# One-hot weights that stand still in the gather of a mixture of experts, and a third early place for its weights

## The chip, the cores and the metric

The kernel runs on one core of a Trainium2 chip. The metric is device time in microseconds (us). A measurement of this kernel is a few executions of the program, and the median is given.

## What is computed

One encoder layer over 256 tokens of width 1024: a projection, a group of gated linear attention heads beside a group of softmax attention heads, an output projection, and then a mixture of experts with 32 experts of which each token takes 4. The part that matters here is the mixture:

```python
h = h + moe_ffn(rms_norm(h, ffn_norm_g), w_router, b_router, w1, b1, w2, b2)
# moe_ffn: top-4 of 32 experts for each token, and for the tokens of expert e
h = xb @ w1[e] + b1[e]                       # xb: gathered tokens; 1024 x 2048 weights
h_glu = minimum(h[:, :1024], 7.0); h_lin = clip(h[:, 1024:], -7.0, 7.0)
act = h_glu * sigmoid(1.702 * h_glu) * (h_lin + 1.0)
y = act @ w2[e] + b2[e]                      # 1024 x 1024 weights, added back with the token's gate
```

All weights are float32. An expert has 12 MB of them, and 32 experts have 403 MB, which is nearly all that the kernel reads.

## The kernel before

It is written by hand, engine by engine, with semaphores. Each engine's program is in the order in which the code emits it.

**The stages.** The front (projection, both attentions, output projection, router) takes about 140 us. Then the 32 experts run one after the other, each for up to 64 tokens (`CAP`). At the end the sum is normalised and stored.

**Weights.** The weights of an expert come in six chunks of 2 MB (128 partitions x 4096 floats, `SLOT`): chunks 0 to 3 are `w1`, chunks 4 and 5 `w2`. Chunks are numbered through, so chunk 6e is the first one of expert e. The tile `ring` has eight slots (`SLOTS`). SyncE (SP) issues all transfers in the order of the chunks. TensorE (PE) counts `chunk_used` up when it has multiplied with a chunk, and SP waits for that count before it loads over a slot. During the front most of the ring holds other things, and SP waits for semaphores of the front before it loads each of the first eight slots (`first_ring`). `EARLY` is the number of chunks that go to a place outside the ring, in the tile `work`, while the front still runs: these are chunks 19 and 20 (`EARLY_AT` is 19). The number of used chunks that SP waits for before it loads chunk c over a slot is c-7 up to chunk 18, c-9 for the chunks 21 to 28 (`SLOTS + EARLY` behind), and c-7 again from chunk 29 on, since the early places are used once (`refill_first`, `PEELED`). From expert 8 on SP loads pairs of chunks (4 MB at a time, L399), each when both chunks before it in its two slots have been used.

**One expert on PE.** `start_hidden` adds the bias. L1642 multiplies the gathered tokens `xg` with four chunks of `w1`: 32 matmuls with 64 columns of stationary operand and 512 columns moving, two matmul instructions for each float32 matmul. Then `gather(n + 1)` fetches the tokens of the next expert (L1544), `combine` adds the result of the expert before (L1556), four transposes turn the hidden values (L1668, they wait for VectorE's `hid_ready`), two turn the gates (L1677), and L1686 multiplies with the two chunks of `w2`, after ScalarE has copied the turned hidden values (`hidT_sb`, L624).

**The gather.** Token rows are split into three bf16 parts (`parts`, `PARTS` is 3) whose sum is the normalised float32 value. For each of 8 blocks of features, 3 parts and 2 tiles of tokens, the part is the stationary operand (128 x 128) and the one-hot matrix of the expert (64 columns) moves: 48 matmuls in bf16. The result stands in bank 6 already turned, with features on the partitions, and VectorE writes it to `xg` with the gain (L1066). The parts are made on ScalarE, VectorE and GpSimd between the router and the first expert (L596, L606, L611, L994, L1006, L1012, L454, L456). `xg` needs features in the order `(m r)` with r running over 4 rows of the weights in one partition (`W1_RUN`), so every use of token rows steps over 4 elements.

**The first gather** is done in two halves (`first_gather`, L1530, and `half_out`, L1074), since the first chunk needs only half of `xg`. It stands ahead of the first L1642 but for its last quarter, which stands behind chunk 0.

## Time and profile before

| | |
|---|---|
| median of 3 runs | 1055.63 us (1055.35 to 1057.44) |
| the profiled execution | 1055.04 us, of which the span of the profile is 1053.3 us |
| PE busy | 985.9 us (94%) |
| VectorE (DVE) busy, ScalarE (ACT) busy | 223.6 us (21%), 119.1 us (11%) |
| read from HBM | 419.95 MB, 400 GB/s over the span |
| granted clock of PE | 0.986 of full speed on average |

Instructions have the line of the program that emits them. Times in views are in us from the start of the span. A view by windows gives the busy time of PE, of PE's weight loads (PEld), DVE, ACT and GpSimd (POOL), the granted clock of PE as a share of full speed, the mean busy share of the 16 DMA engines and what they moved. The chain of work that ended last is followed back from the end of the program; a piece of it is what the piece after it had to wait for.

### The profile page before, as it was taken

The page shows a single profiled execution, that of the slowest core. Times are in us where ns is not written, and L with a number is a line of the kernel's source. Part 1 is how long each engine was busy: PE and PEld are TensorE (multiplying, and loading weights), DVE is VectorE, ACT ScalarE, POOL GpSimd, SP SyncE. Part 2 cuts the span into 40 slices and gives each one's busy share as a digit, 9 for nine tenths or more (in the row PEclk, how much of TensorE's full clock was granted, in tenths as well). Part 3 has the DMA queues.
Part 4 walks back from the last instruction along what each step waited for, and adds up shares of the span by engine and source line. Part 5 has one row for each costly group of instructions (what it writes and reads, how often), then busy time and mean ns, then how long its engine had stood idle before and what let it go on. Part 6 is the DMA issues. An engine that isn't in the chain of part 4 may idle for free.

```text
span 1053.3 us, 13569 instructions
## 1 busy us (share of the span) xinstructions
PE 985.9 (94%) x5863; PEld 438.2 (42%) x5863; DVE 223.6 (21%) x525; ACT 119.1 (11%) x235; POOL 17.3 (2%) x19
## 2 busy tenths in 40 slices
PE   7999999999999999999989899989999889999896
PEld 6646444444343444444333343333343334343332
DVE  1786351111011111111111110111111111010112
ACT  1054130000000000000000000000000000000002
POOL 0010110000000000000000000000000000000000
PEclk9999999999999999999999999999999999999998
DMA  9927769999999999999999999999999999999995
GB/s 356 265 77 320 340 262 430 426 427 423 429 425 433 424 431 428 432 435 424 436 436 424 434 436 426 434 434 429 431 434 433 427 436 434 423 427 427 427 425 205
DMA packets 25233, 421.50 MB, mean 400 GB/s; under 512 B 4176, under 2 KB 4688, under 8 KB 6800
## 3 DMA queue, kind: packets, MB, share of 16 engines
q1 hardware_dynamic: 25200, 421.01, 94.9%
q8 instruction: 26, 0.43, 0.2%
q14 instruction: 7, 0.06, 0.0%
HBM read 419.95 MB, written 1.05 MB: 400 GB/s over the span
## 4 chain that ended last, share of the span: by engine, by line
PE 65%; DMA 30%; ACT 2%; DVE 2%; issue 1%; POOL 1%; SPq 0%; POOLq 0%; DVEq 0%
DMA ring<-in_w_dram 30%; PE bank L1642 29%; PE bank L1686 14%; PE bank L1556 4%; PE bank L1544 3%; PE bank L1206 3%; PE bank L1668 1%; PE bank L1447 1%; PE bank L1278 1%; ACT work L624 1%; PE bank L1375 1%; PE bank L1472 1%; PE bank L1602 1%; PE bank L1247 1%; POOL stat L428 1%
## 5 line engine op out<-in xcount | busy, mean ns | idle before, releaser
L1642 PE MATMUL bank<-ring,work 128*64 128x512 f32 x2016 | 459.7, 608 | 33.1 <-DMA ring<-in_w_dram 33.0
L1642 PEld LDWEIGHTS bank<-ring,work 128*64 128x64 f32 x2016 | 175.8, 139 | 297.0 <-issue 238.1
L1686 PE MATMUL bank<-ring,work 128*64 128x512 f32 x992 | 219.7, 595 | 14.9 <-ACT work L624 14.9
L1090 DVE TENSOR_SCALAR work<-bank 128x512 f32<-128x512 f32 x31 | 21.4, 691 | 685.0 <-PE bank L1642 685.0
L1686 PEld LDWEIGHTS bank<-ring,work 128*64 128x64 f32 x992 | 68.9, 137 | 145.8 <-issue 127.5
L621 ACT ACTIVATE work<-work 128x512 f32<-128x512 f32 x31 | 19.7, 634 | 499.1 <-DVE work L1090 499.1
L1556 PE MATMUL bank<-work 64*128 64x512 f32 x256 | 63.6, 615 | 0.7 <-ACT work L656 0.7
L1544 PE MATMUL bank<-work,tok 128*128 128x64 bf16 x992 | 51.2, 197 | 0.0
L1544 PE MATMUL bank<-work 128*128 128x64 bf16 x496 | 50.0, 197 | 0.0
L1544 PEld LDWEIGHTS bank<-work,tok 128*128 128x128 bf16 x992 | 48.8, 116 | 0.0
L1544 PEld LDWEIGHTS bank<-work 128*128 128x128 bf16 x496 | 36.5, 115 | 24.8 <-issue 24.8
L632 ACT ACTIVATE work<-bank 128x512 f32<-128x512 f32 x31 | 18.5, 597 | 214.7 <-PE bank L1686 214.7
L1556 PEld LDWEIGHTS bank<-work 64*128 64x128 f32 x256 | 22.0, 186 | 18.7 <-issue 15.9
L624 ACT ACTIVATE work<-bank 128x512 f32<-128x512 f32 x31 | 18.5, 597 | 91.6 <-PE bank L1668 91.6
L1668 PEld LDWEIGHTS bank<-ckeep,work 128*128 128x128 f32 x124 | 17.3, 210 | 24.0 <-DVE work L1096 22.5
L1083 DVE TENSOR_SCALAR work<-ckeep,work 128x128 f32<-128x128 f32 x62 | 18.7, 344 | 34.8 <-PE bank L1677 34.8
L428 POOL TENSOR_TENSOR stat<-stat 128x1 f32<-128x1 f32 (+2 forms) x8 | 9.7, 1212 | 955.7 <-DVE stat L683 939.3
L1668 PE MATMUL bank<-ckeep,work 128*128 128x128 f32 x124 | 23.2, 310 | 1.2 <-DVE work L1096 1.2
L1093 DVE SCALAR_TENSOR_TENSOR work<-work 128x512 f32<-128x512 f32 x31 | 21.5, 692 | 1.1
L1096 DVE TENSOR_TENSOR work<-work 128x512 f32<-128x512 f32 x31 | 21.5, 692 | 1.1
L1066 DVE TENSOR_TENSOR work<-bank,ffn_pairs 128x512 f32<-128x512 f32 x31 | 21.2, 683 | 0.0
L1091 DVE TENSOR_SCALAR work<-bank 128x512 f32<-128x512 f32 x31 | 21.1, 680 | 0.0
(221 smaller groups left out, 503.5 us busy)
## 6 DMA issues: line engine op xcount, KB each, us to landing
ring<-in_w_dram SPq DMA_DIRECT2D x60, 4096.0 KB, 29.1
ring<-in_w_dram SPq DMA_DIRECT2D x67, 2048.0 KB, 15.1
ring<-in_w_in_dram SPq DMA_DIRECT2D x8, 1168.0 KB, 15.2
ring<-in_w_dram SPq DMA_DIRECT2D x6, 1024.0 KB, 34.1
work<-in_w_dram SPq DMA_DIRECT2D x2, 2048.0 KB, 14.7
ring<-in_w_out_dram SPq DMA_DIRECT2D x2, 1024.0 KB, 10.5
ring<-in_w_out_dram SPq DMA_DIRECT2D x1, 2048.0 KB, 16.7
h<-in_x_dram SPq DMA_DIRECT2D x2, 512.0 KB, 4.2
```

The lines of the kernel that those rows point to most:

```text
L624: nc.scalar.activation(hidT, bank[5][:, :].rearrange("p (s q) -> p s q", q=P), ACT.Copy)\
L1066: nc.vector.tensor_tensor(xg.rearrange("p (k c) -> p k c", c=CAP), bank[6][:, :].rearrange("p (k c) -> p k c", c=CAP), ffn_pairs.rearrange ...
L1090: nc.vector.tensor_scalar(glu, bank[2][:, :], LIMIT, None, ALU.min).then_inc(S.glu_ready, 1)
L1091: nc.vector.tensor_scalar(lin, bank[5][:, :], LIMIT, -LIMIT, ALU.min, ALU.max).then_inc(S.dve_step, 1)
L1093: nc.vector.scalar_tensor_tensor(lin, lin, 1.0, glu, ALU.add, ALU.mult).then_inc(S.dve_step, 1)
L1096: nc.vector.tensor_tensor(lin, lin, sig, ALU.mult).then_inc(S.hid_ready, 1)
L1206: return mm(o, l, r, start=a and first, stop=z, skip_group_check=True)
L1544: last = mm(bank[6][:, k * CAP:(k + 1) * CAP], rows_of(t, i, k), onehot[:, t, :], start=i == 0 and t == 0, stop=i == PARTS - 1 and t == TI ...
L1556: last = mm(bank[Y[i]][:, :], gatedT[j * CAP:(j + 1) * CAP, t, :], res[j * CAP:(j + 1) * CAP, :], start=start, stop=stop, skip_group_check ...
L1642: last = mm(bank[(2, 5)[g]][j * CAP:(j + 1) * CAP, :], xg[:, k * CAP:(k + 1) * CAP], of_group(chunk[:, r, :], g, j), start=False, stop=k = ...
L1668: last = nc.tensor.transpose(bank[5][:, r * P:(r + 1) * P], apart[:, :, r], ident)
L1686: last = mm(bank[6][j * CAP:(j + 1) * CAP, :], hidT[:, r, s * CAP:(s + 1) * CAP], chunk[:, r, j * 512:(j + 1) * 512], start=s == 0 and r == 0,
```

## The change

The one-hot matrix becomes float32, has the factor 1/rms of each token in its columns, and is now the stationary operand. The float32 token rows `h` move past it, 512 columns at a time: 2 tiles of tokens by 2 halves of the features are 4 float32 matmuls, with tokens of the expert on the partitions of bank 6. ScalarE copies bank 6 to `rows_sb` (the same place as `glu`, so it waits for `hid_ready` too), PE turns it in 4 transposes into bank 2 (`turn_rows`, behind L1677), and VectorE writes `xg` from there. The sigmoid is written to bank 2, and no longer to `sig`. The bf16 parts, and what makes them, are gone.

The place that this frees holds a third early chunk, chunk 21 (`EARLY` is 3), in two halves of 1 MB: one in `tok`, one in `work`. SP loads it behind `first_ring(6)`, after the attention output has been turned (`glaT_ps`). SP now waits for c-10 used chunks before chunk c for the chunks 22 to 29, and for c-7 from chunk 30 on. `TURN` moves the numbering of the slots by one, so that the ring is in step with the pairs. `res`, `gated` and the second half of `hT` move to other places.

```diff
-EARLY = 2
+EARLY = 3
+TURN = 1
+        early_rows = [tok.rearrange("p t d -> p (t d)"), work[:, at_split:at_split + SLOT // W1_ROWS]]
...
         def slot_of(c):
-            return (c - EARLY) % SLOTS
+            return (c - EARLY + TURN) % SLOTS
...
+            def load_split(i):
+                e, r = divmod(EARLY_AT + i, PER_EXPERT)
+                n = SLOT // W1_ROWS
+                for j in range(W1_ROWS):
+                    at = r % PAIR * SLOT + j * n
+                    sp.dma_start(early_rows[j], rows_of(e, r)[:, at:at + n]).then_inc(early_in[i], 16)
...
-            for i in range(EARLY):
+            for i in range(EARLY - 1):
                 load_early(i)
             sp.wait_ge(S.att_used, 1)
             first_ring(6)
+            sp.wait_ge(S.glaT_ps, TILES)
+            load_split(EARLY - 1)
             sp.wait_ge(S.h_ps, 2 * TILES)
             first_ring(7)
...
+            def rows_out(n):
+                act.wait_ge(S.gathered, n + 1)
+                act.wait_ge(S.hid_ready, n)
+                nc.scalar.activation(rows_sb, bank[6][:, :], ACT.Copy).then_inc(S.rows_done, 1)
...
-                nc.scalar.activation(sig, glu, ACT.Sigmoid, scale=ALPHA).then_inc(S.sig_ready, 1)
+                nc.scalar.activation(bank[2][:, :], glu, ACT.Sigmoid, scale=ALPHA).then_inc(S.sig_ready, 1)
+                rows_out(n + 1)
...
             def gathered_out(n):
-                dve.wait_ge(S.gathered, n + 1)
+                dve.wait_ge(S.turned_ps, n + 1)
...
-            left_over(0)
             first_mask(0)
             first_mask(1)
-            last_part(0)
+            half_rows_out()
             half_out(0, 3)
-            left_over(1)
-            last_part(1)
             tables()
...
+            def interleaved(t, nb, r0, n):
+                return h[:, t, nb * 512:(nb + 1) * 512].rearrange("p (m r) -> p r m", r=W1_RUN)[:, r0:r0 + n, :]
...
             def gather(n):
-                for k in range(KD):
-                    for i in range(PARTS):
-                        for t in range(TILES):
-                            last = mm(bank[6][:, k * CAP:(k + 1) * CAP], rows_of(t, i, k), onehot[:, t, :],
-                                      start=i == 0 and t == 0, stop=i == PARTS - 1 and t == TILES - 1)
+                for t in range(TILES):
+                    for j in range(GROUPS):
+                        last = mm(bank[6][j * CAP:(j + 1) * CAP, :], onehot[:, t, :], interleaved(t, j, 0, W1_RUN),
+                                  start=t == 0, stop=t == TILES - 1, skip_group_check=True)
+            def turn_rows(n):
+                pe.wait_ge(S.rows_done, n + 1)
+                for r in range(W1_RUN):
+                    last = nc.tensor.transpose(bank[2][:, r * P:(r + 1) * P], rows_sb[:, r * P:(r + 1) * P], ident)
+                last.then_inc(S.turned_ps, 1)
...
                 last.then_inc(S.gatedT_ps, 1)
+                turn_rows(n + 1)
                 pe.wait_ge(S.hidT_sb, n + 1)
-                pe.wait_ge(S.xg_ready, n + 2)
...
             first_gather(0, 0)
             first_gather(0, 1)
             first_gather(1, 0)
+            turn_first(0)
+            first_gather(1, 1)
```

**PE behind the first layer of expert 1.** Before, from `gather(2)` (L1544, 48 matmuls; of its rows, which repeat in this pattern, the first and the last ones stand here) to the first chunk of `w2`:

```order
L1544 MATMUL bank<-work 128x64 [waits res_ready,xg_ready,onehot_ready]
L1544 MATMUL bank<-work 128x64
L1544 MATMUL bank<-work,tok 128x64 x4
...
L1556 MATMUL bank<-work 128x512 [waits extra_done,res_ready]
L1556 MATMUL bank<-work 128x512 x3
L1668 MATMUL bank<-ckeep,work 128x128 [waits hid_ready]
L1668 MATMUL bank<-ckeep,work 128x128 x3
L1677 MATMUL bank<-ckeep,work 128x128 [waits gatedT_sb,gated_ready]
L1677 MATMUL bank<-ckeep,work 128x128
L1686 MATMUL bank<-ring,work 64x512 [waits slot_in2,xg_ready,hidT_sb]
```

The same stretch of the change, where L1537 is the gather, L1555 `combine` and L1544 the new `turn_rows`:

```order
L1537 MATMUL bank<-h,work 64x512 [waits res_ready,xg_ready,onehot_ready]
L1537 MATMUL bank<-h,work 64x512 x3
L1555 MATMUL bank<-work 128x512 [waits extra_done,res_ready]
L1555 MATMUL bank<-work 128x512 x3
L1668 MATMUL bank<-ckeep,work 128x128 [waits hid_ready]
L1668 MATMUL bank<-ckeep,work 128x128 x3
L1677 MATMUL bank<-ckeep,wr_sb 128x128 [waits gatedT_sb,gated_ready]
L1677 MATMUL bank<-ckeep,wr_sb 128x128
L1544 MATMUL bank<-ckeep,work 128x128 [waits rows_done]
L1544 MATMUL bank<-ckeep,work 128x128 x3
L1686 MATMUL bank<-ring,work 64x512 [waits slot_in3,hidT_sb]
```

48 small matmuls have become 4 large ones, and 4 transposes stand between L1677 and L1686.

**SP at the end of the front.** Before, from the two early chunks to the first refills that wait for `chunk_used`:

```order
L347 DMA work<-in_w_dram 128x4096 [waits ogla_ps]
L347 DMA work<-in_w_dram 128x4096
L347 DMA ring<-in_w_dram 128x4096 [waits att_used]
L347 DMA ring<-in_w_dram 128x4096 [waits h_ps]
L347 DMA ring<-in_w_dram 128x4096 [waits chunk_used] x38
```

The change:

```order
L345 DMA work<-in_w_dram 128x4096 [waits ogla_ps]
L345 DMA work<-in_w_dram 128x4096
L345 DMA ring<-in_w_dram 128x4096 [waits att_used]
L367 DMA tok<-in_w_dram 128x2048 [waits glaT_ps]
L367 DMA work<-in_w_dram 128x2048
L345 DMA ring<-in_w_dram 128x4096 [waits h_ps]
L345 DMA ring<-in_w_dram 128x4096 [waits chunk_used] x37
```

Two transfers of half a chunk come ahead of the last slot of the ring, and one refill fewer waits for `chunk_used`.

**PE at the first gather.** The change, from the filler matmuls (L1470) to the first chunk (L1642); L1518 is `first_gather` and L1527 `turn_first`:

```order
L1470 MATMUL bank<-h,ckeep 128x128 x4
L1518 MATMUL bank<-h,work 64x256 [waits onehot_first]
L1518 MATMUL bank<-h,work 64x256
L1518 MATMUL bank<-h,work 64x256 [waits onehot_ready]
L1518 MATMUL bank<-h,work 64x256
L1518 MATMUL bank<-h,work 64x256 [waits onehot_first]
L1518 MATMUL bank<-h,work 64x256
L1527 MATMUL bank<-ckeep,work 128x128 [waits half_rows]
L1527 MATMUL bank<-ckeep,work 128x128
L1518 MATMUL bank<-h,work 64x256 [waits onehot_ready]
L1518 MATMUL bank<-h,work 64x256
L1642 MATMUL bank<-ring,work 64x512 [waits slot_in1,half_xg]
```

Before, 36 matmuls in bf16 (L1530) stood ahead of the first L1642 and 12 behind chunk 0, and no transposes. Now the second half's two transposes stand behind chunk 0.

## Rows read from the trace of the kernel before

**Rows 1.** The page: busy time by engine, and the chain by engine.

```profile
PE 985.9 (94%) x5863; PEld 438.2 (42%) x5863; DVE 223.6 (21%) x525; ACT 119.1 (11%) x235; POOL 17.3 (2%) x19
...
PE 65%; DMA 30%; ACT 2%; DVE 2%; issue 1%; POOL 1%; SPq 0%; POOLq 0%; DVEq 0%
```

**Rows 2.** Windows: PE, PEld, DVE, ACT, POOL, then PEclk, DMA share, GB/s.

```profile
126.00:134.00 8.00, 8.00 (x43) 4.12 (x45) 3.39 (x7) 3.56 (x7) 1.66 (x3) 1.00 0.03 10
...
140.00:145.00 5.00, 4.67 (x42) 2.04 (x39) 2.67 (x7) 3.13 (x5) 0.00 (x0) 1.00 0.03 11
...
150.00:240.00 90.00, 86.97 (x572) 38.58 (x570) 18.00 (x43) 7.81 (x15) 0.00 (x0) 1.00 1.01 426
```

**Rows 3.** The chain in expert 1: start, us, what.

```profile
168.28 13.79 PE bank L1642 x64
182.07 1.67 PE bank L1544 x48
183.74 1.92 PE bank L1556 x8
185.66 0.69 PE bank L1668 x4
186.38 0.61 ACT work L624
...
187.03 7.09 PE bank L1686 x32
194.11 0.46 PE bank L1472 x4
```

**Rows 4.** The chain where PE waits for weights: two experts apart.

```profile
560.64 7.14 PE bank L1642 x32
...
618.93 7.14 PE bank L1642 x32
```

**Rows 5.** SP's timeline: issues at three places, start and us.

```profile
234.67 0.33 SPq L347 DMA_DIRECT2D ring<-in_w_dram  x1
...
243.30 0.33 SPq L347 DMA_DIRECT2D ring<-in_w_dram  x1
...
361.57 0.33 SPq L399 DMA_DIRECT2D ring<-in_w_dram  x1
```

**Rows 6.** DMA issues: KB, us to landing; windows at 144.5, 234, 243, 361.

```profile
ring<-in_w_dram SPq DMA_DIRECT2D x1, 2048.0 KB, 7.4
...
ring<-in_w_dram SPq DMA_DIRECT2D x1, 2048.0 KB, 12.9
...
ring<-in_w_dram SPq DMA_DIRECT2D x1, 2048.0 KB, 9.1
...
ring<-in_w_dram SPq DMA_DIRECT2D x1, 4096.0 KB, 14.3
```

**Rows 7.** Timeline of expert 1 between its two layers.

```profile
184.15 0.69 DVE L1096 TENSOR_TENSOR work<-work 128x512 f32<-128x512 f32 x1
...
186.18 0.38 PE L1677 MATMUL bank<-ckeep,work 128*128 128x128 f32 x2
...
187.03 1.51 PE L1686 MATMUL bank<-ring,work 128*64 128x512 f32 x6 [0.47 <-ACT work L624]
```

**Rows 8.** Weight loads of L1668 and L1677: ns min/median/max.

```profile
L1668 PEld LDWEIGHTS bank<-ckeep,work x124: 195/209/223, 159.3 to 1007.4; 128*128 128x128 f32 x124
...
L1677 PEld LDWEIGHTS bank<-ckeep,work x62: 141/146/153, 159.8 to 1007.6; 128*128 128x128 f32 x62
```

**Rows 9.** Timeline of the first gather.

```profile
138.31 1.14 PE L1478 MATMUL bank<-h,ckeep 128*128 128x128 f32 x8
...
140.71 0.42 DVE L1074 TENSOR_TENSOR work<-bank,ffn_pairs 128x256 f32<-128x256 f32 x1 [0.42 <-PE bank L1530]
...
141.19 3.71 PE L1642 MATMUL bank<-ring,work 128*64 128x512 f32 x16
```

**Rows 10.** PE's timeline in the last expert.

```profile
1024.29 7.14 PE L1642 MATMUL bank<-ring,work 128*64 128x512 f32 x32 [1.19 <-DMA ring<-in_w_dram]
```

More of the change, by code:

```diff
@@ L219, in encoder_layer @@
         w_out_gla = ring[:, 7 * SLOT:8 * SLOT].rearrange("p (k n) -> p k n", n=D)
-        early = [work[:, KD * SEQ + i * SLOT:KD * SEQ + (i + 1) * SLOT] for i in range(EARLY)]
+        early = [work[:, KD * SEQ + i * SLOT:KD * SEQ + (i + 1) * SLOT] for i in range(EARLY - 1)]
+        at_split = KD * SEQ + (EARLY - 1) * SLOT
+        early_rows = [tok.rearrange("p t d -> p (t d)"), work[:, at_split:at_split + SLOT // W1_ROWS]]
         back = Carve(work)
@@ L240, in encoder_layer @@
         lin = back(FG)
-        sig = back(FG)
-        hidT = back(SUB, P)
-        part0 = back(TILES * D // 2).bitcast(BF16).rearrange("p (t d) -> p t d", d=D)
+        rows_sb = glu
         part_sb = back(TILES, P)
         gateT = part_sb.rearrange("p t c -> p (t c)")
-        res = back(D // GROUPS)
-        reuse = Carve(work, at_glu)
-        left = reuse(TILES, D)
+        hidT = back(SUB, P)
+        left = Carve(work, at_split)(TILES, D)
         assert back.at <= WORK
         b1_wide = tok.rearrange("p t d -> p (t d)")
-        parts12 = tok.bitcast(BF16).rearrange("p t (i d) -> p t i d", i=PARTS - 1)
-        parts = [[part0[:, t, :]] + [parts12[:, t, i, :] for i in range(PARTS - 1)] for t in range(TILES)]
-        hT = [turned[:, :, 0:P], tok[:, 1, :].rearrange("p (k t) -> p k t", t=P)]
+        hT = [turned[:, :, 0:P], Carve(work, at_glu)(KD, P)]
         ffn_pairs = sb("ffn_pairs", [P, KD])
@@ L992, in _ @@
             turned_out(0, 0, 0)
-            dve.wait_ge(S.part0_t0, 1)
-            nc.vector.scalar_tensor_tensor(left[:, 0, :], h[:, 0, :], stat[:, 4:5], parts[0][0], ALU.mult, ALU.subtract)\
-                .then_inc(S.left_t0, 1)
             add_h(1, 1)
@@ L1634, in expert @@
                     fine = final and c in FINE
-                    chunk = by_row(slot_for(q, c) if fine else loaded(q, c, it, final_body), 2 * FF)
+                    chunk = slot_for(q, c) if fine else loaded(q, c, it, final_body)
                     for r in range(W1_ROWS):
@@ L1642, in expert @@
                                 last = mm(bank[(2, 5)[g]][j * CAP:(j + 1) * CAP, :], xg[:, k * CAP:(k + 1) * CAP],
-                                          of_group(chunk[:, r, :], g, j), start=False, stop=k == KD - 1,
+                                          of_group(row_of(chunk, r, 2 * FF), g, j), start=False, stop=k == KD - 1,
                                           skip_group_check=True)
@@ L1686, in expert @@
                             last = mm(bank[6][j * CAP:(j + 1) * CAP, :], hidT[:, r, s * CAP:(s + 1) * CAP],
-                                      chunk[:, r, j * 512:(j + 1) * 512], start=s == 0 and r == 0,
+                                      row_of(chunk, r, D)[:, j * 512:(j + 1) * 512], start=s == 0 and r == 0,
                                       stop=s == W2_CHUNKS - 1 and r == W2_ROWS - 1, skip_group_check=True)
```

127 lines of the change are left out of this document (56 added, 71 removed).

## The prediction

> **What bounds the kernel now.** I read the page first. PE is busy for 94% of the span, and 65% of the chain that ended last is PE and 30% DMA [rows 1]. So neither is the bound alone, and I ask where each is. The windows answer. The DMA engines stand still from 126 to 134 us (share 0.03) and from 140 to 145 us (0.03), and from 150 us on they never do (1.01, 426 GB/s) [rows 2]. Two experts of PE in the second half of the kernel are 618.93 - 560.64 = 58.3 us apart, 29.15 us each or 4.86 us for a chunk of 2 MB [rows 4]. That is the pace of the DMA. PE's own pace is that of expert 1, where it waits for no weights: 13.79 + 1.67 + 1.92 + 0.69 + 0.61 + 0.04 + 7.09 + 0.46 = 26.3 us [rows 3], where 0.04 is the hand-over from ScalarE. So PE is 2.9 us an expert faster than the DMA, lives on what was loaded ahead as long as that lasts, and then waits for weights. The end comes from the DMA: in the last expert PE waited 1.19 us for a chunk, and nothing behind that waits for weights again [rows 10].
>
> From this alone the answer would be simple: every microsecond in which the DMA stands still before 145 us is lost, and the third early place fills 4.86 of them. But a place helps only as long as the DMA always has somewhere to put the next chunk. So I read SP's issues against their landings. The first refill, issued at 144.9 us when the queue is empty [rows 2], lands after 7.4 us [rows 6]; that is 4.86 us of data and 2.5 us around them. The load issued at 234.67 us (chunk 29) lands 12.9 us later, at 247.6, and the one issued at 243.30 (chunk 30) lands 9.1 us later, at 252.4 [rows 5, 6]. The second was issued only 4.3 us before the first had landed. It would have landed as early if issued 9.1 - 7.4 = 1.7 us later, and not more. The ring is nearly full there: SP waited for PE to finish chunk 22. The next narrow place is the pair issued at 361.57 us, which lands after 14.3 us [rows 5, 6]. A pair on an empty queue would take 7.4 + 4.86 = 12.3, so the slack there is 2.0 us. I read all other issues from 170 to 470 us the same way, and all have more. Those of the first expert, before 170 us, have little too, but there the loads themselves will start later (below).
>
> **The change part by part.** *The third place.* It is issued behind the last slot but one and has landed before the last slot is issued: the queue is empty for 8 us from 126 on [rows 2], and 2 MB are 4.86 us. So chunk 21 costs nothing and one refill fewer is left: -4.86 us on the side of the DMA.
>
> *Where that gain meets the ring.* Chunks 22 to 29 now go out at the counts of 21 to 28 before. So chunk 29 lands where chunk 28 did, about 242.7. Chunk 30 still waits for chunk 22 to be used: its count is c-7 before and after. It is issued at 243.30 plus whatever PE has lost by then, and lands 7.4 us later, at 250.7 plus that loss, instead of at 252.4. **So of 4.86 us only 1.7 minus PE's loss remain**, and the DMA stands still for 3 us that it did not before. At 361.57 the same holds with 2.0. What counts is therefore what PE loses in its first four and first eight experts.
>
> *PE's loss in each expert.* The gather: 48 matmuls cost 1.67 us now [rows 3]. It becomes 4 float32 matmuls with 64 stationary columns and 512 moving, the form of L1642 and L1686, 8 instructions. L1642 needs 13.79 / 64 = 0.215 us for each of its instructions, so 8 cost 1.72 us: +0.05. What no row shows is such a matmul whose moving operand steps over 4 floats (16 bytes). The nearest row is L1668, which loads a 128 x 128 operand with this step as weights: 209 ns for one against 146 ns for L1677 without it [rows 8]. But the loads overlap. In pace the step costs little: L1668 begins at 185.66 and L1677 at 186.18 [rows 3, 7], 0.13 us for each of four, or 1.02 ns a column. In L1642 two streams run side by side, so each has 0.43 us for 512 columns, 0.84 ns. At 1.02 the gather costs 4 x 0.52 = 2.09 us: +0.42. I take +0.1, nearer to L1642, since that row is the same form but for the step, and since L1668's pace has the moving of 128 more columns in it.
>
> *The four transposes* stand between L1677 and L1686. By L1668's pace four cost 4 x 0.13 = 0.52 us. PE idles 0.47 us there anyway, waiting for ScalarE's copy L624 [rows 7]. They nearly fit. Their own wait (`rows_done`) is over by then: VectorE's L1096 ends at 184.84 [rows 7], ScalarE's new copy of 0.61 us (the size of L624) ends at 185.5, and the next thing on ScalarE, L624, is due at 186.38 [rows 3]. If the cover went, they would cost 0.52 us. Behind the transposes VectorE has all of L1686 (7.09 us) to write `xg`. I take 0.05 for this, so 0.15 us an expert in all (0.05 to 0.47 by the bounds).
>
> *The first gather.* Removed are the splits into parts, which lie beside PE but for the last one. New are, in line: a copy of 256 columns, two transposes and their hand-overs. L1642's 16 instructions take 3.71 us [rows 9], 0.27 more than 16 x 0.215, which is the drain of the last. So the filler matmuls end their issue at 138.31 + 1.14 - 0.27 = 139.2 [rows 9]. Eight instructions of 256 columns at 0.11 and the drain end at 140.4. The copy (0.42, as L1074), two transposes (0.38, as L1677) and L1074 itself (0.42) with four hand-overs of 0.04 end at 141.8. L1642 began at 141.19 [rows 9], so chunk 0 begins 0.6 us later. Behind it two transposes stand where 12 matmuls did, and a quarter of the gather has moved under L1074: about 0.4 us comes back. 0.2 us is left for the rest.
>
> *Sum.* At the first narrow place PE is 0.2 + 4 x 0.15 = 0.8 us late, so 1.7 - 0.8 = 0.9 us of gain. At the second it is 0.2 + 8 x 0.15 = 1.4 late, so 2.0 - 1.4 = 0.6 us. The smaller one decides: -0.6 us. Later the slack grows by 2.9 us an expert and the loss by 0.15. PE still needs only 26.5 us for an expert, less than the 29.15 of the DMA, and in the last expert the 1.19 us of waiting cover 0.15 [rows 10]. So the profiled execution would go from 1055.04 (span 1053.3 and 1.7 around it) to 1054.4, and the median, 0.6 above the profiled one, from 1055.63 to about 1055.0. 0.2% of this kernel is 2.1 us, about what a measurement can tell from no change.
>
> **The rivals.** *The whole chunk is gained* (chance 0.10). For it: the DMA share is 1.01 all along and the engines stand still at the front [rows 2]. Then the time falls by 4.86 less the 0.6 us by which the first refill is later: 4.3, to 1051.3. Against it stands the pair of issue and landing at 243.30. It needs PE to reach chunk 22 at least 2.6 us earlier than now, and nothing in the change is shorter on PE.
>
> *The stepping operand is slow* (0.18, slower than before). Two streams read the same partitions side by side, each element from another place. If each column pays the 63 ns / 128 = 0.49 ns by which the stepping load is longer [rows 8], one instruction takes 0.43 + 0.25 = 0.68 us and the gather 4 x 0.68 = 2.72 us: +1.05 an expert and +0.3 in the first gather. Then the second narrow place costs 0.5 + 8 x 1.05 - 2.0 = +6.9 us: 1062.5. It decides from 0.23 us an expert on, where 0.2 + 8 x 0.23 = 2.0, and can be measured from 0.5 on. At twice the time for each column it is +1.76 an expert and 12.6 us: 1068. Against it: 48 matmuls of L1544, each with a load of 128 stepping bf16 columns, follow each other at 1.67 / 48 = 0.035 us [rows 3], so PE can read stepping data fast. The Trainium skill has a rule for this, in Advanced Engine Details and Errata, section SBUF Cachelines: accesses that hit the same 16-byte line run at full speed, at least two hits on a line are needed, and another line for each access has a penalty. It gives no size. By that rule the new operand, with one float in each line, would be slow; the longer load in L1668 agrees, its pace hardly.
>
> *The turn is not hidden* (0.10). The transposes come late because ScalarE's copy pushes L624 back, or the hand-overs do not overlap: 0.52 + 0.1 us an expert. 0.2 + 8 x 0.62 - 2.0 = +3.2: 1058.8. Against it: between the end of the copy and L624 there are 0.9 us, by the times above.
>
> **How the numbers follow.** The forecast (the ring is full at chunk 30, PE loses 0.05 to 0.47 an expert) has 0.62, and its own range is 1054.3 to 1057.6: at 0.05 an expert the first place leaves 1.7 - 0.4 = 1.3 of gain and the second 1.4; at 0.47 the second costs 0.2 + 3.8 - 2.0 = 2.0. The range of 8 in 10 is 1053.5 to 1062.5: it leaves out most of the full gain below and the slower half of the stepping operand above. Faster by over 0.2%: 0.10 and 0.02 of the forecast, 0.12. Slower: 0.18 and 0.10 and a little of the forecast, 0.30. Within: 0.58.
>
> **What would show it.** In the profile of the changed kernel the refill on SP near 244 us should be issued to an empty queue (7.4 us to landing), with DMA share near 0.6 for some 4 us there, and full otherwise. The gather should be 8 instructions in 1.7 to 1.9 us, and 2.7 or more if the rival holds. The wait of L1686 for ScalarE should be near 0. PE should begin to wait for weights about one expert later. The prediction is wrong if the DMA never stands still behind 150 us (then the whole chunk is gained), or if one expert of PE takes more than 26.6 us.

## The result, and the profile after

The changed kernel takes 1070.87 us (median of 4 runs, 1070.42 to 1072.33). The kernel before took 1056.24 beside it, so the ratio is 1.0142, with a 95% interval of 1.0130 to 1.0154. I had forecast 1055.0 and a range up to 1062.5. The profiled execution took 1070.75, with a span of 1068.6.

The page of the changed kernel, busy time and the chain by engine:

```profile
PE 1046.7 (98%) x4719; PEld 427.3 (40%) x4719; DVE 224.2 (21%) x521; ACT 133.3 (12%) x262; POOL 13.8 (1%) x17
...
PE 82%; DMA 13%; DVE 2%; SPq 1%; issue 1%; ACT 1%; POOL 0%; POOLq 0%; DVEq 0%
```

PE is busy 61 us longer with 1144 instructions fewer (31 gathers at 1.97 us more, as shown below, make 61), and the chain has moved from the DMA to PE [rows 1]. The chain of one expert says where, in the columns of [rows 3]. L1537 is the gather, L1555 the combine, L1544 the four new transposes, L1464 the next bias rows:

```profile
185.41 3.64 PE bank L1537 x8
189.05 1.92 PE bank L1555 x8
190.97 0.68 PE bank L1668 x4
191.65 0.22 PE bank L1677 x2
191.87 0.44 PE bank L1544 x4
192.30 0.03 issue
192.33 7.09 PE bank L1686 x32
199.42 0.45 PE bank L1464 x4
199.87 13.79 PE bank L1642 x64
```

Line by line against [rows 3]: the gather takes 3.64 us instead of 1.67. L1677 and the new transposes (0.22 + 0.44 + 0.03) stand where the chain went through ScalarE's copy L624 (0.02 + 0.61 + 0.04). All else is as before. One gather begins 28.25 us behind the other (185.41, 213.66), where an expert took 26.3. One row of the view of L1537 (ns min, median, max) shows the size for each instruction; L1642 and L1686, of the same form without the step, have 592:

```profile
L1537 PE MATMUL bank<-h,work x248: 1059/1079/1117, 158.9 to 1022.1; 128*64 128x512 f32 x124
```

The front, that is the chain up to the first expert (L1470 is the filler matmuls, whose result nobody uses, L1518 the first gather, L1527 its transposes):

```profile
138.09 1.76 PE bank L1470 x8
139.86 2.89 PE bank L1518 x12
142.74 0.37 PE bank L1527 x2
143.11 1.03 PE bank L1518 x4
144.15 3.49 PE bank L1642 x16
```

The first matmul of the first expert is at 143.96 (its first records stand under the gather's drain), 2.8 us behind [rows 9].

Now the ring. SP's issues of chunk 30 and of the pair that went out at 361.57 before, then the DMA's view of the two (KB, us to landing), then windows in the columns of [rows 2]:

```profile
252.50 3.76 SPq L345 DMA_DIRECT2D ring<-in_w_dram  x2
...
378.93 0.33 SPq L408 DMA_DIRECT2D ring<-in_w_dram  x1
```

```profile
ring<-in_w_dram SPq DMA_DIRECT2D x1, 2048.0 KB, 7.3
...
ring<-in_w_dram SPq DMA_DIRECT2D x1, 4096.0 KB, 13.0
```

```profile
245.00:250.00 5.00, 4.97 (x26) 2.34 (x26) 0.85 (x2) 1.47 (x3) 0.00 (x0) 1.00 0.00 0
250.00:257.00 7.00, 7.00 (x36) 2.48 (x34) 1.05 (x4) 0.60 (x1) 0.00 (x0) 1.00 0.53 187
```

The DMA engines stand still for some 7 us before 252.5 (the load before landed at 245.7), since the ring is full and PE has not finished chunk 22. Then the load lands 7.3 us after its issue, as on an empty queue [rows 6]. The pair goes out 17.36 us later than in [rows 5] and lands 13.0 us later, at 391.9: 16.1 us behind the kernel before, where it landed at 375.9. In the last expert the same shift stands: the chunk that landed at 1024.2 lands at 1040.3. PE begins with it 16.4 us later than before, at 1040.71 against 1024.29 [rows 10], since PE itself is now 0.4 us behind that landing and no longer waits for it.

### The profile page after: what moved, and what is told of

Same layout as the page of the kernel before. It is cut to its first block, busy times and chain, and to the rows that moved or that the text cites. A ratio compares the mean times of both kernels' runs of the same rounds, so it can differ in the third digit from the quotient of the medians.

```text
span 1068.6 us, 11333 instructions
## 1 busy us (share of the span) xinstructions
PE 1046.7 (98%) x4719; PEld 427.3 (40%) x4719; DVE 224.2 (21%) x521; ACT 133.3 (12%) x262; POOL 13.8 (1%) x17
## 3 DMA queue, kind: packets, MB, share of 16 engines
HBM read 419.95 MB, written 1.05 MB: 394 GB/s over the span
## 4 chain that ended last, share of the span: by engine, by line
PE 82%; DMA 13%; DVE 2%; SPq 1%; issue 1%; ACT 1%; POOL 0%; POOLq 0%; DVEq 0%
PE bank L1642 36%; PE bank L1686 18%; DMA ring<-in_w_dram 11%; PE bank L1537 9%; PE bank L1555 5%; DMA tok<-in_b_dram 2%; PE bank L1668 2%; PE bank L1439 1%; PE bank L1270 1%; PE bank L1464 1%; PE bank L1367 1%; PE bank L1544 1%; PE bank L1602 1%; DVE tok L734 1%; PE bank L1239 1%
## 5 line engine op out<-in xcount | busy, mean ns | idle before, releaser
L1642 PE MATMUL bank<-ring,work 128*64 128x512 f32 x2000 | 440.0, 594 | 3.3 <-DMA ring<-in_w_dram 3.3
L1642 PEld LDWEIGHTS bank<-ring,work 128*64 128x64 f32 x2000 | 176.3, 136 | 247.8 <-issue 231.4
L1686 PE MATMUL bank<-ring,work 128*64 128x512 f32 x992 | 219.7, 595 | 1.4
L1686 PEld LDWEIGHTS bank<-ring,work 128*64 128x64 f32 x992 | 68.8, 137 | 132.2 <-issue 125.3
L1537 PE MATMUL bank<-h,work 128*64 128x512 f32 x248 | 119.2, 1082 | 0.0
L623 ACT ACTIVATE bank<-work 128x512 f32<-128x512 f32 x31 | 18.7, 602 | 457.2 <-DVE work L1084 457.2
L1555 PE MATMUL bank<-work 64*128 64x512 f32 x256 | 63.6, 615 | 0.7 <-ACT work L660 0.7
L1555 PEld LDWEIGHTS bank<-work 64*128 64x128 f32 x256 | 22.0, 186 | 70.1 <-issue 68.5
L1537 PEld LDWEIGHTS bank<-h,work 128*64 128x64 f32 x248 | 24.6, 146 | 58.8 <-issue 58.8
L636 ACT ACTIVATE work<-bank 128x512 f32<-128x512 f32 x31 | 18.5, 598 | 214.7 <-PE bank L1686 214.7
L618 ACT ACTIVATE work<-bank 128x512 f32<-128x512 f32 x31 | 18.5, 597 | 73.7 <-PE bank L1537 73.7
L1668 PEld LDWEIGHTS bank<-ckeep,work 128*128 128x128 f32 x124 | 17.3, 209 | 24.5 <-issue 22.7
L628 ACT ACTIVATE work<-bank 128x512 f32<-128x512 f32 x31 | 18.5, 597 | 60.0 <-PE bank L1668 59.9
L1668 PE MATMUL bank<-ckeep,work 128*128 128x128 f32 x124 | 23.2, 309 | 0.0
L1090 DVE TENSOR_TENSOR work<-work,bank 128x512 f32<-128x512 f32 x31 | 21.3, 687 | 1.1
L1464 PE MATMUL bank<-biases,sel 96*64 96x512 bf16 x128 | 20.0, 390 | 0.0
L1198 PE MATMUL bank<-ring,work 128*128 128x32 f32 (+2 forms) x80 | 19.3, 391 | 0.0
## 6 DMA issues: line engine op xcount, KB each, us to landing
ring<-in_w_in_dram SPq DMA_DIRECT2D x8, 1168.0 KB, 15.3
```

Source lines behind the costliest of these rows:

```text
L1090: nc.vector.tensor_tensor(lin, lin, bank[2][:, :], ALU.mult).then_inc(S.hid_ready, 1)
L1198: return mm(o, l, r, start=a and first, stop=z, skip_group_check=True)
L1464: mm(bank[(2, 5)[g]][j * CAP:(j + 1) * CAP, :], sel, of_group(b1_parts, g, j), start=True, stop=False, skip_group_check=True)
L1537: last = mm(bank[6][j * CAP:(j + 1) * CAP, :], onehot[:, t, :], interleaved(t, j, 0, W1_RUN), start=t == 0, stop=t == TILES - 1, skip_grou ...
L1555: last = mm(bank[Y[i]][:, :], gatedT[j * CAP:(j + 1) * CAP, t, :], res[j * CAP:(j + 1) * CAP, :], start=start, stop=stop, skip_group_check ...
L1642: last = mm(bank[(2, 5)[g]][j * CAP:(j + 1) * CAP, :], xg[:, k * CAP:(k + 1) * CAP], of_group(row_of(chunk, r, 2 * FF), g, j), start=False ...
```

## The experiments

Each run is the changed kernel with one more edit. Times are medians; all ran beside the kernel before, whose medians were 1055.92 to 1056.37 us. That kernel scatters from 1054 to 1061, so I lean on traces where less than 1 us is in question.

### What makes the gather slow

**m1_pace** puts ten groups of eight matmuls behind PE's last instruction. The profile shows an instruction as a record; each matmul gives two records in float32 and one in bf16. One group, shortened (`streams` is 1 or 2, and `moving` picks the columns):

```
for i in range(8):
    j, t = i % streams, i // streams % 2
    mm(bank[5][j * CAP:(j + 1) * CAP, 0:256], weights, moving(t), start=True, stop=True)
```

> The changed kernel with ten groups of eight matmuls behind TensorE's last instruction (their result is not used). Each matmul has 256 columns of moving operand; what varies is whether the columns stand side by side, every second, every fourth or every eighth one (f32 from h, bf16 from the biases), and whether all eight go to the same half of the output partitions (one stream) or alternate between the two halves (two streams). In the changed kernel's gather, f32 with every fourth column and two streams, an instruction of 512 columns takes 0.455 us of the chain, and side by side 0.2155 us: for 256 columns 0.228 and 0.108 us. Theory A, the step slows each stream by itself: f32 step four costs about twice the plain group both with one stream (0.43 to 0.46 us against 0.2155 us an instruction) and with two. Theory B, two streams share one reader that fetches a stepped column in about 0.9 ns: f32 step four costs 0.228 us an instruction with one stream as with two, and one stream loses nothing to plain. Theory C, the step is not the cause (it is reading h in f32, or the one-hot in f32): plain and stepped groups take the same. For the size of the step, A and B both leave open whether step two (8 bytes) lies halfway or with step four, and whether bf16 with step eight (16 bytes) behaves as f32 with step four.

The chain at its end (a count of 15 is a group of 16 records of which one stands in a neighbouring piece). Float32: L1717 and L1720 are side by side with one and two streams, L1723 step two with one stream, L1729 and L1732 step four with one and two. Bf16, one stream: L1735 side by side, L1738 step four, L1741 step eight.

```profile
1061.70 3.38 PE bank L1717 x15
...
1065.30 1.73 PE bank L1720 x15
1067.02 3.40 PE bank L1723 x15
...
1072.47 6.77 PE bank L1729 x15
...
1079.69 3.62 PE bank L1732 x15
1083.32 0.88 PE bank L1735 x8
1084.19 1.81 PE bank L1738 x8
1086.00 3.61 PE bank L1741 x8
```

Divide the second number by the count. Float32 side by side takes 0.225 us a record, step two 0.227, step four 0.451; with two streams 0.115 and 0.241. So theory A holds: the step slows each stream by itself, and two streams still run side by side. Bf16 takes 0.110, 0.226 and 0.451 for spans of 2, 8 and 16 bytes. In one stream that is 0.43, 0.88 and 1.76 ns a column. The granted clock was 1.00 in the stretches of all these groups but the last, where it was 0.94.

**m2_spans** asks how far this goes, with 128 columns and one stream.

> The changed kernel with eleven groups of eight matmuls behind TensorE's last instruction (their result is not used). The first eight groups move 128 columns in one stream: f32 side by side, pairs out of four, step four, eight, sixteen; bf16 step two, four, sixteen. In the earlier trial (256 columns, one stream) a record took 0.226 us for f32 side by side and step two, 0.451 for step four, 0.110 for bf16 side by side, 0.226 for step four, 0.451 for step eight. Theory (a column costs the bytes of row that it spans, about 9 bytes in a ns, and never less than its own pace): pairs of four as plain, 0.113 us; step four 0.225; step eight 0.45 and step sixteen 0.9 us if the span goes on counting; bf16 step two 0.055, step four 0.113, step sixteen 0.9. Rival (from 16 bytes on every column is a fetch of its own at 1.76 ns): step eight and sixteen 0.225 us as step four, bf16 step sixteen 0.225. The last three groups load 128 columns of h as stationary operand, side by side, step four and step eight, and move 64: whether a stepped load slows them as well; from the changed kernel's rows (a load of 209 ns stepped, 146 ns not, for transposes) 0.17 us against 0.11 us a record is expected at most.

L1716 moves pairs out of four, L1718 step four, L1720 step eight, L1722 step sixteen (float32); L1724 step two, L1728 step sixteen (bf16). L1730 and L1734 load h as weights, side by side and with step eight, and move 64 columns.

```profile
1063.38 1.81 PE bank L1716 x16
1065.19 3.63 PE bank L1718 x16
1068.82 3.72 PE bank L1720 x16
1072.53 3.48 PE bank L1722 x16
1076.01 0.46 PE bank L1724 x8
...
1077.40 1.86 PE bank L1728 x8
1079.26 3.40 PE bank L1730 x16
...
1086.38 3.84 PE bank L1734 x16
```

The rival holds: 0.227, 0.232 and 0.217 us for steps of 16, 32 and 64 bytes, so a column costs 1.7 to 1.8 ns in all three. Pairs out of four are as fast as plain (0.113), and so is bf16 with step two (0.058 us for 128 columns, half of 0.110 and a little).

The weights need more care. A stepped load of weights takes 0.24 us a record against 0.21, 13% more, but the granted clock was 1.00 up to 1079.2 us and 0.50, the lower level of 1.2 GHz, from 1080 us on:

```profile
1080.00:1090.00 10.00, 10.00 (x45) 10.00 (x44) 0.00 (x0) 0.00 (x0) 0.00 (x0) 0.50 0.00 0
```

So these groups don't tell what the step costs in the weights at full speed. The next run does: there one load takes 209 ns with the step and 140 without, and four transposes 0.48 us instead of 0.44, 9% more. The moving side pays 100%.

**e1_contiguous** moves the step from the gather to the transposes, in experts 1 to 31 (lines shortened).

```diff
-  mm(bank[6][j * CAP:(j + 1) * CAP, :], onehot[:, t, :], interleaved(t, j, 0, W1_RUN), ...)
+  mm(bank[6][j * CAP:(j + 1) * CAP, :], onehot[:, t, :], h[:, t, j * 512:(j + 1) * 512], ...)
-  nc.tensor.transpose(bank[2][:, r * P:(r + 1) * P], rows_sb[:, r * P:(r + 1) * P], ident)
+  nc.tensor.transpose(bank[2][:, r * P:(r + 1) * P], rows_sb.rearrange("p (m r) -> p r m", r=W1_RUN)[:, r, :], ident)
```

> The changed kernel, but the gather of experts 1 to 31 moves 512 columns of h that stand side by side, and the step of four is in the transposes behind it, which read the picked rows with a step as stationary operand. The first expert's gather still steps. Theory (the stepped moving operand costs the time): the eight gather instructions take 1.72 to 1.80 us of the chain where they took 3.64, the four transposes 0.6 to 0.7 where they took 0.44, an expert on TensorE 26.4 to 26.6 us where it took 28.26, and with 1.6 us lost at the first expert and 8 x 0.2 up to the gate at the pair issue, minus 2.0 of slack, the time is 1056 to 1058 us. Rival (the f32 one-hot or h itself makes the gather slow): the gather stays at 3.6 us and the time at 1070 to 1071.

1057.71 us, ratio 1.0005 (0.9993 to 1.0017). Its chain:

```profile
184.86 1.72 PE bank L1537 x8
...
189.39 0.48 PE bank L1544 x4
...
211.18 1.72 PE bank L1537 x8
```

The gather is back at 1.72, the transposes cost 0.04 more, and an expert takes 26.32 us. One address pattern was 13.2 us of the 14.6.

### Which experts count, and what the third place does then

**e5_first_eight** and **e6_loop_only** are the two halves of e1_contiguous: the quick gather for experts 1 to 8 only, and for 9 to 31 only.

> The gather with columns side by side only for experts 1 to 8, and the stepped one, 3.64 us, for experts 9 to 31. Theory (only TensorE's lag up to the pair issue at 361 us counts; after it TensorE's 28.26 us for an expert is still below DMA's 29.15, so it gains on the weights): the time of the kernel with all gathers side by side, 1056 to 1058, within 0.7 us. Rival (each expert's loss counts, 15.2 us over 31 experts): 22 of 30 stay, some 11 us, and the time is 1066 to 1068.

> The changed kernel with the gather side by side only in experts 9 to 31, and stepped, 3.64 us, for experts 1 to 8: the other half of e5_first_eight. Theory (all of the loss is made before the pair issue at 379): 1070.9 within 0.5 us, though 23 of 31 gathers are twice as fast. Rival (each gather counts): 22 x 1.92 us of 30 x 1.92, or three quarters of the loss, would be gone: 1060 us.

1057.59 and 1069.88. Eight quick gathers give back the whole 13 us. The other 23 give back 1.0, 0.5 more than I had allowed for; 0.4 of it is that PE waits for the last chunks again and is no longer behind them. In e5_first_eight PE goes on at 28.25 us an expert behind expert 8, and that costs next to nothing, since the DMA needs 29.15.

**e3_two_places** has the slow gather and no third place (`EARLY = 2`, `TURN = 0`).

> The changed kernel with its slow gather, but without the third place outside the ring (two as before the change, and the ring begins at the place it began at). Theory (the ring is full from 250 us on, and each refill waits for TensorE's use of the chunk eight before): DMA's turn for chunk 30 comes 4.9 us later than 245.7, at 250.6, and the gate that TensorE opens stands at 252.5, so nothing is lost: 1070.9 within 0.4 us. Rival (the third place is worth a chunk's 4.9 us and the slow gather hides it): 1075 to 1076 us.

1071.10 against 1070.87: the third place is worth nothing in the changed kernel. The DMA stands still anyway (share 0.48 here):

```profile
246.00:254.00 8.00, 7.97 (x40) 3.35 (x40) 1.90 (x6) 1.47 (x3) 0.00 (x0) 1.00 0.48 197
```

### The front

**e2_pairs** lets the first gather read pairs out of four, and its transposes every second picked column. **e7_no_filler** also drops the four filler matmuls ahead of it (lines shortened).

```diff
-  interleaved(t, half, j * RUNS, RUNS)                       # p r m: step of four
+  h[:, t, half * 512:(half + 1) * 512].rearrange("p (m r) -> p m r", r=W1_RUN)[:, :, j * RUNS:(j + 1) * RUNS]
-                if half == 0 and t == 0:
-                    keep_busy(4)
```

> The kernel of e1_contiguous, and the first expert's gather reads pairs of neighbouring f32 columns out of every four instead of single columns with a step of four; its transposes take every second picked column. Theory (a column costs the stretch of row it spans: 0.88 ns for up to 8 bytes, 1.76 ns for 16, in one stream, as the trials with 256 columns gave): a record of 256 columns takes 0.115 to 0.121 us of the chain in place of 0.24, the twelve records before the first transpose 1.4 us in place of 2.84, the first expert begins 1.3 us earlier than in e1_contiguous relative to the front, and the time is 1.3 us below e1_contiguous: 1056.0 to 1056.8 on this chip. Rival A (any column order but one side by side costs double): no change against e1_contiguous. Rival B (what starts the first expert is the copy and the turn, not the gather): under 0.5 us gained.

> The kernel of e2_pairs without the four filler matmuls (eight records, 1.0 us of the chain) ahead of the first gather. In e1_contiguous the one-hot columns of the first token tile stand ready at 139.28, and the gather begins at 140.03, behind the filler. Theory: the first expert begins 0.7 us earlier than in e2_pairs, TensorE's lag at the pair issue behind the kernel before is then some 1.1 us, under the 2.0 us of slack, and the time is about 0.7 us below e2_pairs: 1055.0 to 1056.0, as fast as the kernel before or up to 1 us faster. Rival (the filler holds TensorE's clock): the granted clock falls to 1.2 GHz somewhere in the first expert and the time is that of e2_pairs or longer.

1056.42 and 1055.34 us, ratios 1.0001 (0.9993 to 1.0010) and 0.9995 (0.9985 to 1.0005). The chain of e7_no_filler up to the first expert (L1516 gather, L1061 copy, L1525 transposes, L1640 first layer):

```profile
138.82 1.15 PE bank L1516 x8
139.97 0.02 issue
139.99 0.44 DVE work L1061
140.43 0.04 issue
140.47 0.50 PE bank L1525 x2
140.98 0.60 PE bank L1516 x4
141.58 3.62 PE bank L1640 x16
```

Fronts differ by up to 2 us between executions, so I count from the start of VectorE's step that strikes out the chosen experts (L982 before, L986 after), which stands in all chains: 3.4 us to the first expert before, 6.7 after, 5.9 in e1_contiguous, 4.3 in e2_pairs and 3.6 in e7_no_filler. The filler took 1.76 us in the profiled execution of after and 0.99 in e1_contiguous. That is the clock. The windows of after (PEclk is the third number from the end) show a granted clock of 0.89 and then 0.58 here, so most of the gather ran at the lower level, 1.2 GHz. Below them stand the windows of e7_no_filler, which has no filler and a clock of 1.00, and e10_one_row (below), which has no filler either and 0.53:

```profile
135.00:139.00 4.00, 3.08 (x28) 2.05 (x27) 3.35 (x19) 2.10 (x4) 0.56 (x1) 0.89 0.93 397
139.00:142.00 3.00, 3.00 (x15) 1.64 (x15) 0.11 (x1) 0.00 (x0) 0.00 (x0) 0.58 0.21 90
```

```profile
139.00:142.00 3.00, 2.92 (x22) 1.23 (x22) 1.56 (x6) 0.38 (x1) 0.00 (x0) 1.00 0.42 178
```

```profile
139.00:142.00 3.00, 3.00 (x16) 1.34 (x14) 0.42 (x1) 0.00 (x0) 0.00 (x0) 0.53 0.29 123
```

So the rival of e7_no_filler, that the filler holds the clock, is not refuted by its one trace. Of the eight traces of changed kernels with the filler, one (after) has the lower clock between 139 and 142 us. Of the eight without it, three have (e8_two_places, e9_two_places and e10_one_row: 0.50, 0.65, 0.53), with PE busy for 2.9 of the 4 us ahead, as in most of the others. There the first expert begins 4.7 to 5.0 us behind the shared step and not 3.6. The lower clock takes back what the pairs gained: their first twelve records take 2.83 us in e10_one_row, where twelve stepped ones took 2.84 in e1_contiguous at full clock and 2.89 in after. One trace for each kernel can't tell whether the filler makes this rarer.

### What the third place is worth once PE keeps up

> The kernel of e7_no_filler without the third place outside the ring. Theory (with two places DMA's own turn, not TensorE's use, sets the refills, as in the kernel before, where 2.0 us of slack stood at the pair issue): TensorE's lag of 1.1 us costs nothing, and the time is that of the kernel before, 1056.4 within 0.5 us, which makes the third place worth 2.0 minus 1.1, some 0.9 us, and not 4.9. Rival (the third place is worth a whole chunk): 1060 to 1061 us. Rival (it is worth nothing): the time of e7_no_filler within 0.2 us.

**e7_two_places**: 1055.30, as e7_no_filler. I was wrong by the 0.9 us that I gave the third place. In e7_no_filler the pair goes out at 362.51 and lands 14.1 us later, at 376.6, though the load before landed at 364.85 and a pair on a busy queue takes 9.7: 2.0 us of DMA are lost at this gate (the place where SP waits for PE), all that the third place had left.

**e8_rows_late** moves the four matmuls that add the b2 rows and the four that add h (1.05 us each) from experts 5 and 7 to 28 and 29, behind the gate. **e8_two_places** is the same without the third place.

> The kernel of e7_no_filler, and TensorE's two extra pieces of work in experts 5 and 7 (four matmuls each that add the b2 rows and h to the output sums, 4.2 us of the chain each) are moved behind, to experts 28 and 29, where TensorE waits for weights anyway. In e7_no_filler the load behind the pair issue at 362.40 lands at 376.49, the one before it at 364.75, and a pair takes 9.7 us when DMA never stops: its own turn would be 374.5, so 2.0 us are lost to TensorE's use there. Theory (the third place is worth only what the gates leave, and the gate at 362 takes the rest): TensorE passes the gate 8.4 us earlier, the landing falls to 374.5, and the time is 2.0 us below e7_no_filler, 1053.0 to 1053.8. Rival A (the gates don't matter any more once the first gather is quick; what is left is the end): no change, 1055.3. Rival B (4.2 us in one expert are more than the 2.8 us that TensorE waits there, and the lag of 1.4 to 2.8 us reaches the end): 1055 to 1058.

> The kernel of e8_rows_late without the third place outside the ring. Theory (with two places DMA's own turn sets the landing behind that gate: 366.29 plus 9.7 is 376.0 where e7_two_places landed at 376.13): the earlier TensorE brings 0.1 us only, 1055.0 to 1055.4, so that the third place is worth some 1.5 to 1.9 us in this kernel, where it was worth nothing in e7_no_filler. Rival (the third place brings nothing here either): the time of e8_rows_late within 0.3 us.

1055.68 and 1056.65. The landing behind the gate came 2.1 us earlier, at 374.5, and the last one too (1037.7 against 1039.8), but the median did not move: rival B. PE now waits for no weights from 918 us on, where e7_no_filler waited 5.5 us, so 8.4 us of extra work could not fit. The third place was worth 1.0 us between these two medians, where I had expected 1.5 to 1.9, and e8_two_places stands 1.3 us above its range; in its trace PE is also behind the last chunks, and its first gather ran at the lower clock.

**e9_spread** and **e9_two_places** spread the same work over experts 28 to 30.

> The kernel of e8_rows_late, but the eight extra matmuls (1.05 us each) stand three in expert 28, three in expert 29 and two in expert 30, so that no expert has more than 3.15 us of them beside the 2.8 us that TensorE waits for weights in one. Theory (TensorE's late arrival ate the 2.1 us that DMA's last landing came earlier): TensorE reaches chunk 188 with the landing, 1.2 us earlier than in e8_rows_late, the profiled span falls from 1052.0 to 1050.8 or so, and the median to 1054.4, 1.5 us below the kernel before. Rival (the median of e8_rows_late stood where it did because landings scatter from run to run, and TensorE's lag had no part in it): 1055.7, as e8_rows_late.

> The kernel of e9_spread without the third place outside the ring. Theory (with both gates behind TensorE, the third place is worth the 1.4 us by which the last landing of e8_rows_late, 1037.6, lay before that of e8_two_places, 1039.0): 1.4 us above e9_spread, 1055.8. Rival (it is worth nothing at the end): the time of e9_spread within 0.3 us.

1055.88 and 1057.23: a miss for the time of both, though their difference, 1.35, is the 1.4 that I had expected. I had read the wait of one expert where the sum of all that is left counts, and work that stands later leaves less time to catch up. In e9_spread PE reached chunk 188 at 1025.88, 3.1 us behind its landing. (The 1039.0 in that text was read against a wrong zero. It is 1040.4, in an execution whose front was 1.2 us later; counted from the first expert on, the two last landings are 1.5 us apart. Some other landings in these texts are off by 0.1.)

**e10_one_row** moves the b2 rows only, 4.2 us, to expert 28.

```diff
-  rows=add_row if n == BIAS_AT else add_h if n == RESIDUAL_AT else None     # written experts
+  rows=add_h if n == RESIDUAL_AT else None
+  rows=add_row if q == 0 else None                                          # last four experts
```

> The kernel of e7_no_filler, and only the four matmuls that add the b2 rows (4.2 us in expert 5) are moved behind, to expert 28; those that add h stay in expert 7. TensorE passes the gate of the pair issue 4.2 us earlier, more than the 2.1 us that the landing behind it gained in e8_rows_late, and has 4.2 us more behind 918 us, where e7_no_filler waits 5.5 us for weights. Theory (the third place is worth up to 2 us when no gate and no late TensorE takes it back): the landing behind the gate at about 374.4, the last landing 1037.6, TensorE's last chunk begins at 1037.1 where e7_no_filler's began at 1039.2, the span of a typical execution is 2 us below e7_no_filler's, and the median 1053.5 to 1054.3. Rival (something else takes it back again): 1055.3 to 1056.

> The kernel of e10_one_row without the third place outside the ring. Theory: 1.4 to 1.8 us above e10_one_row, 1055.2 to 1055.8, the time of e7_two_places. Rival (the third place is worth nothing): the time of e10_one_row within 0.3 us.

**1053.24 us, ratio 0.9968 (0.9956 to 0.9979)**, and 1054.82 without the third place, ratio 0.9985 (0.9975 to 0.9995). This is faster than the kernel before and the changed one. Both medians are 0.3 to 0.4 us under the ranges that I had given, and their difference, 1.6 us, is inside its range. It rests on the medians alone: the two profiled executions have the same span, 1051.8, the one with two places being the fastest of its eleven, and the one with three having the lower clock in its first gather. PE's waits from 918 us on, in e7_no_filler and then in e10_one_row (us in total, times, longest):

```profile
PE bank L1640 <- DMA ring<-in_w_dram: 5.5, 5, 1.8
```

```profile
PE bank L1640 <- DMA ring<-in_w_dram: 1.4, 2, 1.2
```

1.2 us of those 1.4 are the wait in the last expert: PE is again there ahead of the last chunks. And the pair, issued at 358.53, is no longer late for the DMA: it lands 17.0 us later, at 375.5, 9.7 behind the one before.

**b_again** is the kernel before, with a second profile.

> The kernel before, unchanged, a second time with a profile. Between the profiled executions of before and after, TensorE's last chunk shifts by 16.4 us and the span by 15.3; the output's last write ends 4.2 us behind the last instruction of ScalarE in before and 3.1 us in all changed kernels. If that is a property of the kernel before, it shows 4.2 us again; if it is chance of one execution, it shows 3.1 us. Likewise for the landing behind the pair issue at 361.58 (14.3 us), which the estimate of 2.0 us of slack rested on.

The 14.3 us of the pair are 14.4 again. So is the end: ScalarE's last instruction, in the chain of before and of after,

```profile
1048.40 0.72 ACT tok L669
```

```profile
1064.77 0.72 ACT tok L673
```

ends 4.1 us ahead of the span's end in before and in b_again, and 3.1 in after and in all its variants. The change takes 1.0 us off the end: the output's last write lands 3.3 us behind its issue before and 2.3 after. Why, no run tells.

## Why the prediction was wrong

- **The size of PE's loss in the gather** failed, and it made the miss. I took +0.1 us an expert and bounded it at +0.42; it is +1.97. The error was in the choice of rows. I priced the stepped moving operand by L1668, whose stepped operand is loaded as weights [rows 8], and set its 1.02 ns a column against 0.84 for one of two streams. But L1668 is one stream, and its step is in the weights: with it four transposes take 9% longer (0.48 us against 0.44, e1_contiguous against after). The moving operand pays 100%, in each of two streams. No row of before showed that form, and I called a bound what was a guess from the other operand. L1544's 48 quick matmuls [rows 3], which I held against the rival, have their step in the weights too.
- **The stepping operand is slow**, the rival of 0.18, was right, and nearest at "twice the time for each column": +1.76 an expert and 1068. The Trainium skill (Advanced Engine Details and Errata, section SBUF Cachelines) wants at least two hits on a 16-byte line and gives no size for the penalty. In float32 the runs agree with it: two hits (step two) take 0.227 us, as fast as plain, and one hit (step four) 0.451. In bf16 they do not: two hits on a line (step four) cost twice the plain time in m1_pace, and the measurement decides.
- **The first gather** was mis-sized: +0.6 us for chunk 0, +0.2 in the sum; it was +2.8. Counted from the shared step it is 3.3: 0.8 the lower clock in this execution, which is luck, 1.6 the step (e1_contiguous to e2_pairs), 0.7 the filler, which lay beside the splits before and which I left on the path without asking whether the mask was ready sooner, and 0.25 the copy and the turn.
- **The ring is full** was right, place for place: chunk 30 waits for chunk 22, lands 7.3 us after its issue, the DMA stands still before it and the whole chunk is not gained. "Some 4 us" became 7, since PE was 9 us late there and not 0.8.
- **The slack of 2.0 us at the pair** was too large. I took 12.3 us for a pair on an empty queue; the changed kernel shows 13.0, so at most 1.3 us are slack. In e7_two_places PE was 0.9 us later at this gate and the landing 0.3, so about half a microsecond is nearer. The forecast of a gain needed the 2.0: with 1.3 of slack and the 1.4 of loss that I forecast, nothing is gained.
- **The form of the sum** was right: first loss, eight experts, minus slack. With what was measured, expert 1 begins 3.3 us late (171.62 against 168.28): 2.8 for the first gather, less 0.2 that come back behind chunk 0, and 0.75 in expert 0. That is not 1.97, since before PE waited there 2.8 us for VectorE (156.49 to 159.31) and the quick gather stood in that wait and cost nothing; the sum took this gather in full. Seven more at 1.97 are 13.8, which makes 17.1 of the 17.4; the rest stands in experts 5 and 7. The landing is 16.1 late, and the difference is the 1.3 of slack. e5_first_eight and e6_loop_only show that the experts behind the eighth hardly count.
- **The turn is hidden** was right: 0.44 us of transposes in 0.47 us of idle time, and L1686 waits for nothing.
- **The end** was not in the sum at all: -1.0 us, so 16.4 on PE became 15.3 in the span. The medians are 14.6 apart, since the profiled execution of before was 1.2 us faster than its median and that of after only 0.1.
- **The whole chunk is gained** is refuted by e3_two_places. With the gates open the third place gives 1.6 us by the medians (e10_one_row against e10_two_places), not 4.86. Chunk 30 lands at 251.9 with it and at 253.8 without, 1.8 us apart, so the idle stretch ahead of that chunk keeps the rest.

## What to carry to other kernels

Ask for each operand of a matmul separately how it is read: put a step into the weights, where it costs little here (0.04 us for four transposes), and keep the span of a moving column within 8 bytes in float32 and 4 in bf16. Where a buffer is full, an earlier load is worth only what the next gate leaves, so look for work that can move behind that gate, of the engine for which the loads wait, and count the idle time that is left behind it as one sum. And price an operation that the trace doesn't have by rows that use the same operand in the same way, or call its cost open.

## What the runs showed of the hardware

At full clock and in one stream a moving operand costs by the span of one column (m1_pace, m2_spans): 0.43 to 0.45 ns for bf16 with a span of 2 or 4 bytes, 0.88 ns for 8 bytes, 0.88 and 0.89 ns for float32 with 4 and 8, and 1.76 ns for 16 bytes in both, with 1.7 to 1.8 at 32 and 64. Columns 8 bytes wide in pairs out of four are free for float32. Two streams side by side, on the two halves of the output partitions, each keep their own pace (a record every 0.241 us for two with step four, against 0.451 for one). At 1.2 GHz the step could not be told from no step: twelve stepped records of the first gather took 2.89 us in after, most of them at that clock, and twelve of pairs 2.83 in e10_one_row. Only these steps were tried: between 8 and 16 bytes nothing was.
